# Memory projection of a transformer step on one NeuronCore: VectorE instead of GpSimd adds the squares of the residual, and two intermediate tiles move to PSUM

## The chip, the cores and the metric

The kernel runs on one core of one Trainium2 chip. A core has TensorE (PE) for matmuls, VectorE (DVE) and ScalarE (ACT) for element-wise work, GpSimd (POOL), and SyncE (SP), which here only issues DMAs. Each works through its own queue in order, and they meet at semaphores. SBUF is the working memory, PSUM holds the matmul results in eight banks of 128 x 512 float32. The metric is the device time of one execution in microseconds (us); lower is better. The kernel before takes 2259.66 us, the median of 3 runs (2257.73 to 2259.71).

## The reference

Two transformer blocks run in sequence over 512 tokens of width 1024, all in float32. The change touches one place in the second block: the end of its mixer and the start of its memory cross-attention.

```python
y = hybrid_mixer(rmsnorm_2(h, g[0]), ...)
h = h + rmsnorm_2(y, g[1])                                  # the new residual
y = memory_cross_attention(rmsnorm_2(h, g[2]), rmsnorm_2(mem, mem_norm_g[l]), ...)

def memory_cross_attention(h, mem_n, w_q, w_kv, w_o):
    q = (h @ w_q)                                           # phase "xq"
    k, v = jnp.split(mem_n @ w_kv, 2, axis=-1)              # phase "kv"
    ...

def rmsnorm_2(x, g):
    return x * lax.rsqrt(jnp.mean(x * x, axis=-1, keepdims=True) + EPS) * g
```

The mean of squares runs over the 1024 features of a token. The kernel holds activations as 8 feature tiles of 128 partitions x 512 tokens, so it squares 8 tiles, adds them into one tile (`sqacc`), and lets matmuls against a column of ones sum over the partitions.

## The kernel before

All weights stream from HBM as 324 units of 128 x 1024 float32 (512 KB), four buffers deep (`RING`). Each product is made of three matmuls of split numbers: a weight `w` is split into `w_hi`, which ScalarE writes (`split_hi`, helper line 529), and `w_lo = raw - w_hi`, which GpSimd writes (`split_lo`, line 468). TensorE takes a unit only when its `w_lo` is there (`weights`, line 1715, semaphore `lo_ready`). ScalarE makes `w_hi` of a unit three units ahead, after TensorE has finished the one whose buffers it takes.

The stage in question is phase `kv`, the projection of the 256 memory tokens: 16 units, called 0 to 15 below. Units 0 to 7 give the keys, one feature tile per unit, 24 matmuls of 256 columns (lines 2271 to 2274). Units 8 to 15 give the values, 12 matmuls of 512 columns per unit (`token_tiles`); `stat()` stands between units 11 and 12 and sums `sqacc` over the partitions, and `spread_rs()` behind unit 15 spreads the inverse root. Then phase `xq` begins, eight units of 24 matmuls of 512 columns on the new residual.

While TensorE runs units 0 to 15, the other engines make the new residual out of the mixer's output `yv`, tile by tile, k = 0 to 7:

- VectorE, `next_residual` (lines 1304 to 1326): scales `yv` by gain and inverse root (line 1319), adds it to `resid` (1320), and one tile later writes `x_lo` of the normalised input's low part (`low`, 1311) out of `resid` and `x_hi`.
- ScalarE, `scaled_tile` (558 to 563): writes `x_hi`, then squares the residual tile, into `sqacc` for k = 0, otherwise into one of two halves of `tn`. Between them in its queue it makes `w_hi` and moves the key tile out of PSUM (`kmt`, line 911).
- GpSimd (lines 511 to 519): makes `w_lo` of units 3 to 11, with one `add_square` (line 455, `sqacc += tn`) after each of the splits from unit 5 on, and at last raises `sq_ready`, for which `stat()` waits.

The order on each engine is the order in which the code is written. Two waits tie them: a square for k of 3 or more waits until the square two tiles back is added (`rsq_used`), and ScalarE's last `scaled_tile` waits for all the additions (line 563) before it goes on to `w_hi` of unit 12. The same GpSimd loop `add_squares` is used at two other places of the program, which the change leaves alone.

Of the kernel before, what the change touches and what calls it, by code (L numbers as in the profile page):

```python
# [36 lines left out]
ALU = mybir.AluOpType  # L37
ACT = mybir.ActivationFunctionType
# [4 lines left out]
KT = D // P  # L43
T = 512
# [3 lines left out]
RING = 4  # L48
AHEAD = RING - 1
# [120 lines left out]
U0, N_UNITS = starts(PHASES)  # L170
# [31 lines left out]
def build_program(nc, dram):  # L202
    ctx = ExitStack()
    with ctx:
# [18 lines left out]
        resid = fixed("resid", (P, KT, T))  # L223
# [22 lines left out]
        sqacc = fixed("sqacc", (P, T))  # L246
# [94 lines left out]
        aux = ctx.enter_context(nc.psum_tensor("aux", [P, 6 * T], F32))  # L341
        rs = aux[:, 5 * T:6 * T]
# [5 lines left out]
        def sem(name):  # L348
# [5 lines left out]
        S = {n: sem(n) for n in (  # L354

            "dve_step", "act_step", "pool_step",
            "decay_free", "decay_loaded", "consts_loaded", "x_loaded", "tables_loaded", "consts_ready", "stored",
            "ada0_loaded0", "ada0_loaded1", "ada0_loaded2", "ada0_loaded3", "ada1_loaded", "ada_used",
            "ada_ready", "c_ready_act",
            "sq_ready", "stat_ready", "root_ready", "recip_ready", "rs_ready", "res_ready", "rsq_ready", "rsq_used",  # L360
            "hs_ready", "hrecip_ready", "tap_ready", "tap_used", "normed", "norm_hi", "x_ready",
            "v_ready", "z_ready", "log_ready", "sp_ready", "sp_hi_ready", "sp_split",
# [84 lines left out]
        def _(pool):  # L447
            step = Count(pool, S["pool_step"])
            rsq, used = Count(pool, S["rsq_ready"]), Count(pool, S["rsq_used"])

            def add_square(k):

                rsq.next()
                if k:
                    used.own(nc.gpsimd.tensor_tensor(sqacc[:], sqacc[:], tn[:, k % 2, :], ALU.add))  # L455
                if k == KT - 1:
                    pool.sem_inc(S["sq_ready"], 1)
# [7 lines left out]
            def split_lo(u):  # L465
                s = u.slot(RING)
                pool.wait_ge(hi_ready, (u + 1).val())
                nc.gpsimd.tensor_tensor(w_lo[s][:], raw[s][:], w_hi[s][:].bitcast(F32),  # L468
                                        ALU.subtract).then_inc(lo_ready, 1)

            def split_units(first, end):
                with pool.Fori(0, (end - first) // RING) as i:
                    for j in range(RING):
                        split_lo(At(first + j, i, RING))
# [12 lines left out]
            pool_taps, added = list(POOL_TAPS), [0]  # L487
# [22 lines left out]
            split_units(U0["mix_out"] + RING, U0["kv"])  # L510
            for j in range(AHEAD):
                split_lo(At(U0["kv"] + j))
            for k in range(KT):
                split_lo(At(U0["kv"] + AHEAD + k))
                if k:
                    add_square(k - 1)
            split_lo(At(U0["kv"] + AHEAD + KT))
            add_square(KT - 1)
            split_units(U0["kv"] + AHEAD + KT + 1, U0["up"])
            next_phase(U0["up"], NU)  # L520


# [1 line left out]
        def _(act):  # L524
            step = Count(act, S["act_step"])
            own = {n: Count(act, S[n]) for n in S}
# [25 lines left out]
            def square_tile(k):  # L552

                if k >= 3:
                    own["rsq_used"].next()
                own["rsq_ready"].own(f(tn[:, k % 2, :] if k else sqacc[:], resid[:, k, :], ACT.Square))

            def scaled_tile(k, gain):
                own["res_ready"].next()
                own["norm_hi"].own(f(x_hi[:, k, :], resid[:, k, :], scale=gain[:, k:k + 1]))  # L560
                square_tile(k)
                if k == KT - 1:
                    own["rsq_used"].next(2)

# [170 lines left out]
            for j in range(24):  # L735
# [4 lines left out]
                if j in next_hi:  # L740
                    k = next_hi[j]
# [242 lines left out]
        def _(dve):  # L984
# [319 lines left out]
            def next_residual(y, gain, x_gain):  # L1304


                own["rs_ready"].next()

                def low(k):
                    own["norm_hi"].next()  # L1310
                    own["x_ready"].own(V.scalar_tensor_tensor(x_lo[:, k, :], resid[:, k, :], x_gain[:, k:k + 1],
                                                              x_hi[:, k, :].bitcast(F32), ALU.mult, ALU.subtract))

                for k in range(KT):
                    if y is None:
                        own["res_ready"].own(V.scalar_tensor_tensor(resid[:, k, :], resid[:, k, :], gain[:, k:k + 1], rs,
                                                                    ALU.mult, ALU.mult))
                    else:
                        step.own(V.scalar_tensor_tensor(y[:, k, :], y[:, k, :], gain[:, k:k + 1], rs, ALU.mult, ALU.mult))
                        own["res_ready"].own(V.tensor_tensor(resid[:, k, :], resid[:, k, :], y[:, k, :], ALU.add))  # L1320
                    if k:
                        low(k - 1)
                low(KT - 1)
                own["sq_ready"].skip()
                invert()
                take_rs()
# [1147 lines left out]
```

## Time and profile before

| | |
|---|---|
| time, median of 3 runs | 2259.66 us |
| profiled execution | 2259.86 us, span 2257.7 us |
| mean granted TensorE clock | 0.969 |
| TensorE busy | 2097.1 us (93% of the span) |
| GpSimd busy | 945.8 us (42%) |
| VectorE busy | 989.9 us (44%) |
| ScalarE busy | 921.7 us (41%) |
| chain that ended last | PE 81%, DVE 9%, ACT 5%, issue 2%, POOL 2% |

The profile is one execution, and its times are from the span's start; the stage lies at about 1641 to 1701 us. Busy shares are averages over the whole program, so they say little about a stage of 60 us; what is read there is who waits for whom. An instruction's row shows its start, its length, its engine and line, and in square brackets how long the engine sat idle before it and what ended that. Line 529 is the helper through which ScalarE's operations go, so they are told apart by their tiles.

### The profile page before, as it was taken

Reading aid. Unit: us, or ns where it says so; the run is one execution under the profiler, and the core shown is the slowest. Engines: PE = TensorE matmul, PEld = TensorE weight load, DVE = VectorE, ACT = ScalarE, POOL = GpSimd, SP = SyncE. Lnnn points to the kernel's source line nnn. Section 1 sums busy time; section 2 is a strip of 40 time slices with the busy share of each in tenths; the row PEclk is TensorE's granted clock in tenths of the full one; section 3 lists DMA queues with packets and bytes.
Section 4 is the critical chain, followed back from the end, with each engine's and each line's share of the span. In section 5 each row is a group of like instructions: output and inputs, shape, how many; then the busy total and the mean of one; then the engine's idle time right before and its main releaser. Section 6 shows DMA issues by size and latency. Waiting matters only on the chain.

```text
span 2257.7 us, 27865 instructions
## 1 busy us (share of the span) xinstructions
PE 2097.1 (93%) x9954; PEld 1719.7 (76%) x9954; DVE 989.9 (44%) x1101; ACT 921.7 (41%) x1094; POOL 945.8 (42%) x431
## 2 busy tenths in 40 slices
PE   3999989999999998999999999888889869999996
PEld 3788868787878777888888878787678557887885
DVE  7055532454544556211124377484661364343223
ACT  2366652223232342444422475563352325555421
POOL 3422224243434333444445376572374043444451
PEclk9999999999999999999999999898999979999998
DMA  7311112433333322323333222100333022232331
GB/s 266 94 57 57 57 56 86 153 107 132 116 133 130 111 83 76 93 93 102 93 103 102 87 73 72 50 1 1 119 105 122 10 65 66 93 96 91 111 102 46
DMA packets 56232, 203.69 MB, mean 90 GB/s; under 512 B 6240, under 2 KB 6368, under 8 KB 55904
## 3 DMA queue, kind: packets, MB, share of 16 engines
q1 hardware_dynamic: 56160, 202.70, 27.8%
q8 instruction: 49, 0.80, 0.1%
q14 instruction: 23, 0.19, 0.0%
HBM read 200.57 MB, written 2.10 MB: 90 GB/s over the span
## 4 chain that ended last, share of the span: by engine, by line
PE 81%; DVE 9%; ACT 5%; issue 2%; POOL 2%; DMA 1%; DVEq 0%; ACTq 0%; SPq 0%; POOLq 0%
PE acc L1719 21%; PE acc L1721 20%; PE acc L1720 20%; PE aux L1719 2%; PE aux L1721 2%; PE aux L1720 2%; ACT sp L529 2%; PE acc L1928 2%; PE aux L1776 2%; PE aux L2152 1%; DVE cfy L1375 1%; PE aux L1783 1%; POOL sqacc L455 1%; PE aux L1842 1%; PE acc L2311 1%
## 5 line engine op out<-in xcount | busy, mean ns | idle before, releaser
L468 POOL TENSOR_TENSOR w_lo<-raw,w_hi 128x1024 fp32r<-128x1024 f32 x324 | 796.1, 2460 | 1192.4 <-ACT w_hi L529 1190.9
L1719 PE MATMUL acc<-x_hi,w_hi 128*128 128x512 f32 x1544 | 618.2, 400 | 12.7 <-DVEq L994 3.8
L1720 PE MATMUL acc<-x_lo,w_hi 128*128 128x512 f32 x1544 | 607.3, 393 | 0.0
L1721 PE MATMUL acc<-x_hi,w_lo 128*128 128x512 f32 x1544 | 606.6, 393 | 0.0
L529 ACT ACTIVATE w_hi<-raw 128x1024 fp32r<-128x1024 f32 x324 | 342.7, 1060 | 555.3 <-PE acc L1721 441.1
L1719 PEld LDWEIGHTS acc<-x_hi,w_hi 128*128 128x128 f32 x1544 | 294.1, 190 | 87.7 <-issue 9.1
L1721 PEld LDWEIGHTS acc<-x_hi,w_lo 128*128 128x128 f32 x1544 | 293.5, 190 | 63.1
L1720 PEld LDWEIGHTS acc<-x_lo,w_hi 128*128 128x128 f32 x1544 | 294.0, 190 | 58.8
L529 ACT ACT_TABLE_LOAD x86 | 110.3, 1283 | 54.5 <-DVE tn L1678 20.8
L1678 DVE SCALAR_TENSOR_TENSOR tn<-acc,cols,tn 128x511 f32<-128x511 f32 x88 | 65.9, 749 | 122.1 <-ACT tn L529 115.7
L1025 DVE SCALAR_TENSOR_TENSOR adac<-ada,c_act,adac 128x1024 f32<-128x1024 f32 x42 | 65.7, 1564 | 97.4 <-DMA ada<-in_ada 96.5
L1247 DVE TENSOR_TENSOR ht<-acc,tn 128x512 f32<-128x512 f32 x22 | 15.2, 692 | 182.4 <-PE acc L1721 178.6
L499 POOL TENSOR_TENSOR cfy<-cfy,tn 128x512 f32<-128x512 f32 x48 | 67.0, 1396 | 36.6 <-ACT tn L529 34.5
L1719 PE MATMUL aux<-w_hi,x_hi 128*128 128x512 f32 x192 | 76.1, 396 | 6.5 <-DVE x_lo L1053 5.2
L1720 PE MATMUL aux<-w_lo,x_hi 128*128 128x512 f32 x192 | 75.7, 394 | 0.0
L1721 PE MATMUL aux<-w_hi,x_lo 128*128 128x512 f32 x192 | 75.7, 394 | 0.0
L1719 PE MATMUL acc<-g_hi,w_hi 128*128 128x512 f32 x176 | 69.3, 394 | 0.0
L1719 PE MATMUL acc<-h_hi,w_hi 128*128 128x512 f32 x176 | 69.3, 394 | 0.0
L1721 PE MATMUL acc<-g_hi,w_lo 128*128 128x512 f32 x176 | 69.0, 392 | 0.0
L1721 PE MATMUL acc<-h_hi,w_lo 128*128 128x512 f32 x176 | 69.0, 392 | 0.0
L1720 PE MATMUL acc<-h_lo,w_hi 128*128 128x512 f32 x176 | 68.3, 388 | 0.0
L1720 PE MATMUL acc<-g_lo,w_hi 128*128 128x512 f32 x176 | 68.3, 388 | 0.0
(376 smaller groups left out, 3228.1 us busy)
## 6 DMA issues: line engine op xcount, KB each, us to landing
raw<-in_weights SPq DMA_DIRECT2D x324, 512.0 KB, 3.5
ada<-in_ada SPq DMA_DIRECT2D x48, 512.0 KB, 3.6
resid<-in_x SPq DMA_DIRECT2D x1, 2048.0 KB, 11.7
out<-resid SPq DMA_DIRECT2D x8, 256.0 KB, 2.0
decay<-in_tables SPq DMA_DIRECT2D x4, 256.0 KB, 3.6
memf<-in_mem SPq DMA_DIRECT2D x1, 1024.0 KB, 4.9
angles<-in_tables SPq DMA_DIRECT2D x1, 512.0 KB, 3.5
small<-in_small SPq DMA_DIRECT2D x1, 320.0 KB, 3.8
```

Of the source, the lines that this page charges most:

```text
L455: used.own(nc.gpsimd.tensor_tensor(sqacc[:], sqacc[:], tn[:, k % 2, :], ALU.add))
L468: nc.gpsimd.tensor_tensor(w_lo[s][:], raw[s][:], w_hi[s][:].bitcast(F32), ALU.subtract).then_inc(lo_ready, 1)
L499: tap_used.own(nc.gpsimd.tensor_tensor(cfy[:, n, :], cfy[:, n, :], product(tap_used.at.c), ALU.add))
L529: return nc.scalar.activation(out, in_, func, **kw)
L1025: return V.scalar_tensor_tensor(dst[:], w, c, dst[:], ALU.mult, ALU.add)
L1375: ins = V.scalar_tensor_tensor(y, x, w, y, ALU.mult, ALU.add)
L1678: ins = V.scalar_tensor_tensor(y, bank(t)[:, 0:T - d], w, y, ALU.mult, ALU.add)
L1719: M(out, a_hi, b_hi, start=first, stop=False)
L1720: M(out, a_hi, b_lo, start=False, stop=False)
L1721: return M(out, a_lo, b_hi, start=False, stop=last)
L1776: m = M(aux[:, at_ + b:at_ + b + 1], src[:, b * P:(b + 1) * P], ones[:, 0:1], start=k == 0 and b == 0, stop=k == len(sources) - 1, skip_gr ...
L1928: m = M(bank(t)[:, j * P:T], rv[:, j, e * P:(e + 1) * P], rsc[:, a:a + w], start=j == 0, stop=j == NB - 1)
```

## The change

Four edits, all for this one stage:

1. GpSimd no longer adds the squares: its queue holds only splits in the stage, and its counters skip the semaphores' values.
2. VectorE adds them, in `low(k)`, behind the write of `x_lo`: seven `tensor_tensor` into `sqacc`. It raises `sq_ready` after the last.
3. ScalarE writes the squares for k of 1 and more into PSUM, banks 2 and 3 of `aux` in turn, not into `tn` in SBUF. Its waits are the same, now on VectorE's additions.
4. The scaled output goes to PSUM bank 4 of `aux` (`added`), not back into `yv` in SBUF, and the addition to `resid` reads it there.

```diff
@@ gpsimd
-            for k in range(KT):
-                split_lo(At(U0["kv"] + AHEAD + k))
-                if k:
-                    add_square(k - 1)
-            split_lo(At(U0["kv"] + AHEAD + KT))
-            add_square(KT - 1)
-            split_units(U0["kv"] + AHEAD + KT + 1, U0["up"])
+            rsq.skip(KT)
+            used.skip(KT - 1)
+            split_lo(At(U0["kv"] + AHEAD))
+            split_units(U0["kv"] + RING, U0["up"])
@@ scalar, scaled_tile
-                square_tile(k)
+                if k >= 3:
+                    own["rsq_used"].next()
+                own["rsq_ready"].own(f(aux[:, (2 + k % 2) * T:(3 + k % 2) * T] if k else sqacc[:], resid[:, k, :], ACT.Square))
@@ vector, next_residual
+                own["rsq_ready"].skip(KT)
+                own["rsq_used"].skip(KT - 1)
+                added = aux[:, 4 * T:5 * T]
 
                 def low(k):
                     own["norm_hi"].next()
                     own["x_ready"].own(V.scalar_tensor_tensor(x_lo[:, k, :], ...))
+                    own["rsq_ready"].next()
+                    if k:
+                        own["rsq_used"].own(V.tensor_tensor(sqacc[:], sqacc[:], aux[:, (2 + k % 2) * T:(3 + k % 2) * T], ALU.add))
...
-                        step.own(V.scalar_tensor_tensor(y[:, k, :], y[:, k, :], gain[:, k:k + 1], rs, ALU.mult, ALU.mult))
-                        own["res_ready"].own(V.tensor_tensor(resid[:, k, :], resid[:, k, :], y[:, k, :], ALU.add))
+                        step.own(V.scalar_tensor_tensor(added, y[:, k, :], gain[:, k:k + 1], rs, ALU.mult, ALU.mult))
+                        own["res_ready"].own(V.tensor_tensor(resid[:, k, :], resid[:, k, :], added, ALU.add))
...
                 low(KT - 1)
+                V.sem_inc(S["sq_ready"], 1)
                 own["sq_ready"].skip()
```

GpSimd's queue in the stage before, from unit 5 on (`w_lo_58` is the low half of unit 5, and the numbers 57 to 60 are the four buffers in turn):

```order
L468 TENSOR_TENSOR w_lo_58<-raw_50,w_hi_54 128x1024
L455 TENSOR_TENSOR sqacc<-sqacc,tn 128x512
L468 TENSOR_TENSOR w_lo_59<-raw_51,w_hi_55 128x1024
L455 TENSOR_TENSOR sqacc<-sqacc,tn 128x512
L468 TENSOR_TENSOR w_lo_60<-raw_52,w_hi_56 128x1024
L455 TENSOR_TENSOR sqacc<-sqacc,tn 128x512
L468 TENSOR_TENSOR w_lo_57<-raw_49,w_hi_53 128x1024
```

The same place now, where a loop of four splits runs from unit 4 on:

```order
L468 TENSOR_TENSOR w_lo_57<-raw_49,w_hi_53 128x1024
L467 REGISTER_ALU
L468 TENSOR_TENSOR w_lo_58<-raw_50,w_hi_54 128x1024
L467 REGISTER_ALU
L468 TENSOR_TENSOR w_lo_59<-raw_51,w_hi_55 128x1024
L467 REGISTER_ALU
L468 TENSOR_TENSOR w_lo_60<-raw_52,w_hi_56 128x1024
```

Seven additions are gone from between the splits; register work of the loop stands there in their place.

VectorE's queue before, from the residual tile k = 1 on:

```order
L1319 SCALAR_TENSOR_TENSOR yv<-yv,cols,aux 128x512
L1320 TENSOR_TENSOR resid<-resid,yv 128x512
L1311 SCALAR_TENSOR_TENSOR x_lo<-resid,cols,x_hi 128x512
L1319 SCALAR_TENSOR_TENSOR yv<-yv,cols,aux 128x512
L1320 TENSOR_TENSOR resid<-resid,yv 128x512
L1311 SCALAR_TENSOR_TENSOR x_lo<-resid,cols,x_hi 128x512
L1319 SCALAR_TENSOR_TENSOR yv<-yv,cols,aux 128x512
L1320 TENSOR_TENSOR resid<-resid,yv 128x512
```

And now (the line numbers are those of the changed kernel, in which these operations are lines 1325, 1326, 1313 and, new, 1318):

```order
L1325 SCALAR_TENSOR_TENSOR aux<-yv,cols,aux 128x512
L1326 TENSOR_TENSOR resid<-resid,aux 128x512
L1313 SCALAR_TENSOR_TENSOR x_lo<-resid,cols,x_hi 128x512
L1325 SCALAR_TENSOR_TENSOR aux<-yv,cols,aux 128x512
L1326 TENSOR_TENSOR resid<-resid,aux 128x512
L1313 SCALAR_TENSOR_TENSOR x_lo<-resid,cols,x_hi 128x512
L1318 TENSOR_TENSOR sqacc<-sqacc,aux 128x512
L1325 SCALAR_TENSOR_TENSOR aux<-yv,cols,aux 128x512
L1326 TENSOR_TENSOR resid<-resid,aux 128x512
```

A turn of VectorE has four instructions instead of three from k = 2 on, and `x_lo` is the only one of them left with both tile operands in SBUF.

## Rows read from the trace of the kernel before

**Rows 1.** Chain that ended last: start, length, work.
```profile
1682.46 1.70 POOL sqacc L455
1685.37 2.36 POOL w_lo L468
```

**Rows 2.** Waits, 1639 to 1702: waiting work, releaser, total us, times, longest.
```profile
ACT w_hi L529 <- POOL sqacc L455: 4.3, 1, 4.3
PE aux L1719 <- POOL w_lo L468: 7.0, 5, 1.4
PE acc L1719 <- POOL w_lo L468: 1.1, 1, 1.1
```

**Rows 3.** TensorE in order of time: start, length, instruction, idle before.
```profile
1663.31 0.28 PE L1721 MATMUL acc<-mem_hi,w_lo 128*128 128x256 f32 x1
...
1669.07 0.50 PE L1719 MATMUL aux<-w_hi,mem_hi 128*128 128x512 f32 x1 [1.33 <-POOL w_lo L468]
...
1685.42 0.95 PE L1776 MATMUL aux<-small,sqacc 128*128 128x1 f32 x8
1687.77 0.50 PE L1719 MATMUL aux<-w_hi,mem_hi 128*128 128x512 f32 x1 [1.41 <-POOL w_lo L468]
...
1695.02 0.40 PE L1719 MATMUL aux<-w_hi,mem_hi 128*128 128x512 f32 x1
...
1697.82 0.40 PE L1719 MATMUL aux<-w_hi,mem_hi 128*128 128x512 f32 x1
...
1700.62 1.05 PE L1783 MATMUL aux<-small,rcol 128*128 128x128 f32 x8
1701.42 0.47 PE L1719 MATMUL acc<-x_hi,w_hi 128*128 128x512 f32 x1
```

**Rows 4.** Busy time by stretch; the number behind POOL is the granted clock.
```profile
1646.40:1663.40 17.00, 17.00 (x146) 16.98 (x145) 16.25 (x13) 12.13 (x18) 12.57 (x6) 1.00 0.36 120
...
1689.07:1692.26 3.19, 3.19 (x9) 2.51 (x8) 0.00 (x0) 0.32 (x1) 3.19 (x2) 0.50 0.71 190
```

**Rows 5.** GpSimd in order of time.
```profile
1655.43 1.76 POOL L455 TENSOR_TENSOR sqacc<-sqacc,tn 128x512 f32<-128x512 f32 x1
1657.27 2.74 POOL L468 TENSOR_TENSOR w_lo<-raw,w_hi 128x1024 fp32r<-128x1024 f32 x1
...
1703.27 2.40 POOL L468 TENSOR_TENSOR w_lo<-raw,w_hi 128x1024 fp32r<-128x1024 f32 x1 [1.46 <-ACT w_hi L529]
```

**Rows 6.** ScalarE in order of time.
```profile
1652.84 0.37 ACT L529 ACTIVATE kmt<-acc 128x256 f32<-128x256 f32 x1
...
1654.07 0.63 ACT L529 ACTIVATE tn<-resid 128x512 f32<-128x512 f32 x1
1654.74 1.06 ACT L529 ACTIVATE w_hi<-raw 128x1024 fp32r<-128x1024 f32 x1
1655.71 0.36 ACT L529 ACTIVATE kmt<-acc 128x256 f32<-128x256 f32 x1
```

**Rows 7.** VectorE in order of time.
```profile
1646.74 0.75 DVE L1319 SCALAR_TENSOR_TENSOR yv<-yv,cols,aux 128x512 f32<-128x512 f32 x1 [5.01 <-PE aux L1783]
1647.52 2.90 DVE L1320 TENSOR_TENSOR resid<-resid,yv 128x512 f32<-128x512 f32 x1
...
1651.96 0.75 DVE L1311 SCALAR_TENSOR_TENSOR x_lo<-resid,cols,x_hi 128x512 fp32r<-128x512 f32 x1
```

**Rows 8.** Tiles of VectorE: line, form, count: shortest/median/longest ns, first and last start.
```profile
L1320 DVE TENSOR_TENSOR resid<-resid,yv x8: 692/1974/2899, 1647.5 to 1676.6; 128x512 f32<-128x512 f32 x8
L1311 DVE SCALAR_TENSOR_TENSOR x_lo<-resid,cols,x_hi x8: 751/1672/2732, 1652.0 to 1680.3; 128x512 fp32r<-128x512 f32 x8
L1319 DVE SCALAR_TENSOR_TENSOR yv<-yv,cols,aux x8: 748/748/749, 1646.7 to 1675.8; 128x512 f32<-128x512 f32 x8
L1531 DVE TENSOR_TENSOR xm<-xm,aux x20: 686/689/690, 1462.7 to 1514.3; 128x512 f32<-128x512 f32 x20
L1449 DVE TENSOR_TENSOR acc<-acc,spare x12: 699/700/700, 1329.5 to 1414.4; 128x512 f32<-128x512 f32 x12
```

## The prediction

> **What bounds the kernel now.** I read the chain of waits first: from 1653 to 1688 us it does not run over TensorE but over GpSimd, where a split and an addition of squares follow each other [rows 1]. The waits say who pays: TensorE stood 7.0 us in five waits and 1.1 us in a sixth for `w_lo`, and ScalarE once 4.3 us for the last addition [rows 2]. Outside this stage the change moves nothing, so the question is how much earlier phase `xq` can begin than at 1701.42 us [rows 3].
>
> GpSimd's period before is one split and one addition. A split alone takes 2.40 us and an addition 1.76, but split and addition in turn take 2.74 + 1.76, 4.5 us together [rows 5]: the split is stretched by 0.34. VectorE shows the other half of the same thing. Where both tile operands are in SBUF, an instruction of 0.69 or 0.75 us takes 1.97 or 1.67 in the median; where one is in PSUM (lines 1319, 1531), shortest and longest differ by at most 4 ns [rows 8]. So the two engines shut each other out, and only for operations with two SBUF operands.
>
> TensorE needs a unit every 2.8 us. Units 8 to 15 are 12 matmuls each, and between 1695.02 and 1697.82 lie twelve: 2.80 us. Units 1 to 6 fill 1646.4 to 1663.43 (the last matmul starts at 1663.31, and they follow at 0.12): 2.83 each. 4.5 us of GpSimd against 2.8 of TensorE is why TensorE starves once its lead of three units is used up, at 1663.43.
>
> **The ceiling of the gain.** If TensorE never waited after 1663.43, unit 7 would take 2.83, units 8 to 15 8 x 2.80 = 22.40, the sum over partitions 0.95 and the spreading 0.80 (1700.62 to 1701.42) [rows 3]. That is 26.98 us, and `xq` would begin at 1690.4, 11.0 us earlier. Of the 11.0, 1.65 is not waiting: from unit 12 to the spreading it took 12.85 us where 11.20 do, because from 1689.07 to 1692.26 the granted clock was 0.50, the 1.2 GHz level, just after the row of waits. With TensorE full from 1646.4 to 1663.4 it was 1.00 [rows 4]. I count it as gained, since the waits ahead of it go.
>
> **The change part by part.**
>
> *GpSimd.* Seven additions of 1.76 go, and their stretching of the splits in part. What is left is one split per unit: 2.40 alone, 2.74 when VectorE is in the way, both under 2.80. The loop's register work stands between splits at 1703.27 too, and the split there is 2.40 [rows 5]; I cost it at nothing, its cover being some 2.5 us of lead per unit.
>
> *ScalarE.* Its turn in the stage is 2.87 us, kmt to kmt [rows 6], so now it and TensorE (2.83) set the pace together; 0.04 a unit over seven units is 0.3 us, inside the lead. Its squares now land in PSUM, which no row before shows for ScalarE. The same square into SBUF takes 0.63. As ends I take 0.36, the key tile with half the columns, and 1.06, the `w_hi` with twice the columns [rows 6], and as value 0.63, the row of the same operation. At 0.36 nothing changes in the layout below, at 1.06 `xq` begins 1.8 us later.
>
> *VectorE.* Its turn becomes scale 0.75, add to the residual 0.69, `x_lo` 0.75, add square 0.69, and four gaps of 0.03 to 0.04: 3.0 us. The form "SBUF and PSUM in, SBUF out" takes 0.69 (line 1531), "PSUM out" 0.70 (line 1449) [rows 8]. For the scaling, which now also writes PSUM, the ends are 0.70 (line 1449, which does so) and 0.76 (its own 0.75 and the 0.01 by which 1449 lies above 1531), and the value is 0.75. The residual's addition loses its waits, 1.97 to 0.69; `x_lo` keeps its own.
>
> *Laid out from 1646.74*, when VectorE gets the inverse root [rows 7]: eight turns of 3.02 less the missing addition of square 0 end at 1670.2. Added are the waits that remain: `x_lo` 0 waits 0.9 for ScalarE's `x_hi`; `x_lo` 1 asks in the middle of the split of unit 5 and waits 1.2; `x_lo` 7 asks just after the split of unit 11 has begun and waits 1.4; small ones make 0.4. The last addition ends at 1674.1, where it was 1684.15. `x_lo` 2 to 6 fall into the 0.4 us between two splits, unit by unit.
>
> *The wait that takes the old one's place.* ScalarE holds the `w_hi` of unit 12 until the last addition is done. From there: `w_hi` 1.06, split 2.40, hand-overs 0.2, in all 3.7, so TensorE has unit 12 at 1677.8. It wants it at 1663.43 + 2.83 + 4 x 2.80 + 0.95 = 1678.4. The margin is 0.6 us: this is the tight place, and every microsecond that the last addition is later than 1674.7 is lost one for one. For the units before, the split is ready 2.4 to 2.8 us ahead of TensorE. `stat()` itself wants the additions only at 1677.4.
>
> *Downstream.* `xq` and all behind it begin earlier by the same amount and find the same state. The last splits before `xq` (unit 16 is wanted at 1690.4) end at 1687.5.
>
> *Sum.* 11.0 less 0.6, for one of the turns that just miss a gap between splits (a miss costs up to 2.4 us there, but it moves the last `x_lo` out of its own wait of 1.4): 10.4 us. The profiled execution took 2259.86 us, its span 2257.7; 2259.86 - 10.4 = 2249.5. The median is 0.2 under the profiled execution: 2249.3.
>
> A page of the Trainium skill speaks against the change: "VectorE: DVE Perf Modes", section "The TRN2 errata", has a VectorE operation cost 58 cycles plus its elements from SBUF and 120 plus its elements from PSUM, at 0.96 GHz. This case's trace does not agree for two-operand forms: 689 ns with PSUM (line 1531), 692 for the shortest with none (line 1320) [rows 8]. By the page the two additions of a turn would take 0.755 each and the time would be that of the first rival.
>
> **The rivals.**
>
> *Longer turns, missed gaps.* If the additions on PSUM take 0.75, as the scaling does, not 0.69, a turn is 3.15 against ScalarE's 2.87. VectorE then falls out of the gap between two splits at `x_lo` 4 and again at 6, waits out a split each time, and the last addition ends at 1677.4. Unit 12 starts at 1681.1, 2.7 late: gain 8.3, time 2251.4. The far end is a lock-step: ScalarE waits for the residual tile, its `w_hi` ends 2.5 later, the split 2.5 after that, and `x_lo` waits for that split. A turn P then satisfies P = (5.0 - P) + 0.75 + 0.69 + 0.75 + 0.69 + 0.1, so P = 4.0; eight turns end at 1678.7, unit 12 starts at 1682.4: gain 7.0, 2252.7. For it: GpSimd is busy 2.4 of 2.87 us, so a gap is small. Against it: the forms of [rows 8].
>
> *The time is given back.* TensorE's faster pace wants 512 KB every 2.8 us. If the weights came later than ScalarE asks, the gain would go. To cancel it within the bound of no change they would have to be over 6 us late, and a load is released when the split of four units before is done, about 8 us before its `w_hi` is due. Or ScalarE's writes to PSUM are dearer than the end that I took. Time about 2257.
>
> *Slower: operands in PSUM do not free VectorE.* If an addition with one operand in PSUM still waits for GpSimd, the residual's addition and the square's stay at 1.97. Then every turn waits out one split: 3.0 + 2.4 = 5.4 us, eight turns from 1646.74 end near 1690, unit 12 starts at 1694.6, `xq` at 1694.6 + 11.2 + 0.8 = 1706.6: 5.2 later than before, 2264.9. It decides from a turn of about 4.8 us on, where unit 12 starts at 1689. For it: seven more instructions on VectorE, and the median of 1.97 before. Against it: the 28 executions of lines 1319 and 1531 within 4 ns, those of 1319 in this very stage [rows 8].
>
> **How the numbers follow.** The forecast has 0.72: `xq` at 1690.4 to 1692.0 and perhaps a half-clock stretch that stays (1.65), which is 2248.4 to 2251.2. Longer turns 0.16 (2251.2 to 2254.5), given back 0.07, slower 0.05. The range is 2247.4 to 2254.5, with a microsecond of spread between runs below; it leaves out the two last cases. About 0.2%, 4.5 us, is what a measurement of this kernel can tell from no change: faster 0.88, same 0.07, slower 0.05.
>
> **What would show it.** In the changed profile: GpSimd has no addition between 1650 and 1690 and its splits come every 2.8 to 2.9 us; the residual's addition is 0.69 to 0.70 in all eight; `x_lo` is still stretched, in two or three of eight; TensorE has no wait for `w_lo` in units 7 to 11, and at unit 12 none or under 1 us; the granted clock stays 1.00 from 1646 to the end of the stage; `xq` begins at 1690.4 to 1692. It is wrong if TensorE waits at unit 12 for more than 1.5 us (the margin is mis-sized), if the residual's addition is stretched (the slower rival), or if ScalarE's square is over 0.9 us.

## The result, and the profile after

The changed kernel takes 2245.26 us, the median of 4 runs (2244.34 to 2246.15); the kernel before took 2258.69 in 4 runs (2257.33 to 2259.71) that include the three shown above. The ratio is 0.994, 95% interval 0.9924 to 0.9955: the interval lies wholly under 1, so the change is faster by 0.6%, small but clear of noise. The time lies 4.0 us under the forecast of 2249.3 and 2.1 under the range's lower end. The profiled execution took 2246.15, its span 2244.3; before it was 2259.86 and 2257.7. One run of the kernel before, at 7381.75 us where all others lie between 2253 and 2263, is left out of every figure below.

TensorE in order of time, as in [rows 3] (start, length, instruction, idle before):

```profile
1676.39 0.50 PE L1726 MATMUL aux<-w_hi,mem_hi 128*128 128x512 f32 x1 [0.27 <-POOL w_lo L468]
...
1687.69 1.05 PE L1790 MATMUL aux<-small,rcol 128*128 128x128 f32 x8
1688.50 0.47 PE L1726 MATMUL acc<-x_hi,w_hi 128*128 128x512 f32 x1
```

This is the only wait for `w_lo` that is left, 0.27 us at unit 12, where six waits made 8.1 us [rows 2]. The stage, from the scaling that starts it to `xq`'s first matmul, goes from 54.68 us (1646.74 to 1701.42) to 44.04 (1644.46 to 1688.50). The stretches of the stage show no half clock (the number behind POOL is the granted clock; compare 0.50 in [rows 4]):

```profile
1644.40:1661.40 17.00, 17.00 (x147) 17.00 (x146) 14.68 (x19) 13.99 (x21) 12.42 (x5) 1.00 0.46 146
1661.40:1676.40 15.00, 14.73 (x81) 12.47 (x79) 10.90 (x13) 10.36 (x16) 10.35 (x6) 1.00 0.46 144
1676.40:1688.50 12.10, 12.10 (x56) 9.88 (x57) 0.18 (x1) 5.41 (x7) 12.10 (x6) 1.00 0.65 205
```

VectorE's tiles, as in [rows 8] (here shortest/median/longest ns):

```profile
L1326 DVE TENSOR_TENSOR resid<-resid,aux x8: 686/686/687, 1645.2 to 1669.0; 128x512 f32<-128x512 f32 x8
L1313 DVE SCALAR_TENSOR_TENSOR x_lo<-resid,cols,x_hi x8: 752/752/2914, 1648.5 to 1671.3; 128x512 fp32r<-128x512 f32 x8
L1325 DVE SCALAR_TENSOR_TENSOR aux<-yv,cols,aux x8: 754/756/756, 1644.5 to 1668.2; 128x512 f32<-128x512 f32 x8
L1318 DVE TENSOR_TENSOR sqacc<-sqacc,aux x7: 686/686/689, 1653.3 to 1672.0; 128x512 f32<-128x512 f32 x7
```

The residual's addition fell from 1974 ns in the median to 686, and its longest is 1 ns above its shortest. Only `x_lo`, which still reads two SBUF tiles, is stretched, and only in two of eight:

```profile
1651.41 1.82 DVE L1313 SCALAR_TENSOR_TENSOR x_lo<-resid,cols,x_hi 128x512 fp32r<-128x512 f32 x1 [0.60 <-ACT x_hi L526]
...
1664.56 2.91 DVE L1313 SCALAR_TENSOR_TENSOR x_lo<-resid,cols,x_hi 128x512 fp32r<-128x512 f32 x1
...
1672.04 0.69 DVE L1318 TENSOR_TENSOR sqacc<-sqacc,aux 128x512 f32<-128x512 f32 x1
```

The last addition ends at 1672.73, 28.3 us after the start of the stage, where it took 37.4. ScalarE, as in [rows 6]:

```profile
1650.10 0.36 ACT L526 ACTIVATE kmt<-acc 128x256 f32<-128x256 f32 x1
...
1651.34 0.60 ACT L526 ACTIVATE aux<-resid 128x512 f32<-128x512 f32 x1
...
1652.94 0.37 ACT L526 ACTIVATE kmt<-acc 128x256 f32<-128x256 f32 x1
```

**Where 13.7 us of the profiled execution went.** The stage gives 10.64. It also began 2.28 earlier, though nothing ahead of it was edited; what follows `xq`'s first matmul took 555.80 instead of 556.28, 0.48 less; and the time outside the span is 0.31 less. The last three were in no term of the forecast; e1, e2, e10 and e11 ask whether they belong to the change.

### The profile page after: what moved, and what is told of

It is laid out like the page before. It is cut to its first block, busy times and chain, and to the rows that moved or that the text cites. A ratio compares the mean times of both kernels' runs of the same rounds, so it can differ in the third digit from the quotient of the medians.

```text
span 2244.3 us, 27877 instructions
## 1 busy us (share of the span) xinstructions
PE 2091.8 (93%) x9954; PEld 1716.7 (76%) x9954; DVE 980.2 (44%) x1108; ACT 921.4 (41%) x1094; POOL 933.1 (42%) x424
## 4 chain that ended last, share of the span: by engine, by line
PE 80%; DVE 9%; ACT 5%; issue 3%; POOL 2%; DMA 1%; DVEq 0%; ACTq 0%; SPq 0%; POOLq 0%
PE acc L1726 21%; PE acc L1728 20%; PE acc L1727 20%; PE aux L1726 2%; PE aux L1728 2%; PE aux L1727 2%; ACT sp L526 2%; PE acc L1935 2%; PE aux L1783 1%; PE aux L2159 1%; DVE cfy L1382 1%; POOL w_lo L468 1%; PE aux L1790 1%; PE aux L1849 1%; DMA ada<-in_ada 1%
```

## The experiments

Each kernel was timed beside the kernel before, except the last two, which are single profiled executions. e1 to e4 ran on one chip, e5 to e8 on a second, e9 to e11 on a third; the kernel before had medians of 2258.2, 2257.7 and 2258.7 there. "Stage" is measured as above. In the edits shown, `...` stands for lines left out.

### e1 and e2: both kernels again

No edit.

> The kernel before, unchanged, as a second program. The stage gain explains 10.6 of the 13.4 us (from the arrival of the inverse root to the start of phase xq 54.7 us before, 44.0 after); 2.3 us more were already there when the stage began, in code that the change leaves alone. Theory A (executions differ by themselves): this kernel is within 0.1% of the kernel before, and its profile begins the stage at a time other than 1646.7, by up to 2.5 us either way, through half-clock stretches and DMA waits that lie elsewhere; its stage is still 54.0 to 55.0 long. Rival B (the change shifts the whole program for good): its profile begins the stage at 1646.7 +- 0.3.

> The changed kernel, unchanged, beside the same runs. Theory A: the difference in time lies between 10.6 and 13.4 us and its profile may begin the stage anywhere from 1644.4 to 1647; stage 44.0 +- 0.3 long. Rival B: the difference is 13.0 to 13.8 again and the stage begins at 1644.4 +- 0.3 again.

Measured: the kernel before again 2258.64 us (12 runs, 2254.34 to 2262.98), ratio 1.0006 [0.9997, 1.0015]; the changed kernel 2246.83 (5 runs, 2244.5 to 2248.75), ratio 0.9955 [0.9942, 0.9968]. Stages 54.73 and 44.06, within 0.05 of the first profiles; the wait at unit 12 is 0.29. The stage starts at 1649.96 and 1644.58. The first is not rival B's 1646.7, but it is 3.2 us away from it where theory A had up to 2.5, and the kernel before is again the later of the two, so e10 and e11 ask once more. The stage reproduces to hundredths, and the whole does not: all 71 runs of the kernel before, those of the later experiments included, lie between 2252.99 and 2262.98, with median 2258.19, and 9 of the changed one between 2244.34 and 2248.75, median 2246.15. The difference of these medians is 12.0.

### e3: VectorE adds, both tiles stay in SBUF

```
-  own["rsq_ready"].own(f(aux[:, (2 + k % 2) * T:(3 + k % 2) * T] if k else sqacc[:], resid[:, k, :], ACT.Square))
+  own["rsq_ready"].own(f(tn[:, k % 2, :] if k else sqacc[:], resid[:, k, :], ACT.Square))
...
-  own["rsq_used"].own(V.tensor_tensor(sqacc[:], sqacc[:], aux[:, (2 + k % 2) * T:(3 + k % 2) * T], ALU.add))
+  own["rsq_used"].own(V.tensor_tensor(sqacc[:], sqacc[:], tn[:, k % 2, :], ALU.add))
...
-  step.own(V.scalar_tensor_tensor(added, y[:, k, :], gain[:, k:k + 1], rs, ALU.mult, ALU.mult))
-  own["res_ready"].own(V.tensor_tensor(resid[:, k, :], resid[:, k, :], added, ALU.add))
+  step.own(V.scalar_tensor_tensor(y[:, k, :], y[:, k, :], gain[:, k:k + 1], rs, ALU.mult, ALU.mult))
+  own["res_ready"].own(V.tensor_tensor(resid[:, k, :], resid[:, k, :], y[:, k, :], ALU.add))
```

> VectorE adds the squares, but squares and scaled output stay in SBUF (tn and yv). Theory (homes matter: every VectorE operation with two SBUF operands waits for GpSimd's split): the residual addition and the square addition are stretched to about 2 us in the median, a turn is about 5 us, and the stage is no shorter than before: laid out with the durations of the trace, xq begins 1.3 us later than before; time -3 to +4 us against the kernel before. Rival (what counts is only that GpSimd's queue has no additions): at least 8 us faster than before.

Measured: 2259.67 (11 runs), ratio 1.001 [1.0, 1.0019]; stage 58.08, 3.4 longer than before. Three rows of its trace, GpSimd and VectorE in order of time, and one of TensorE:

```profile
1666.49 2.48 POOL L468 TENSOR_TENSOR w_lo<-raw,w_hi 128x1024 fp32r<-128x1024 f32 x1 [0.33 <-ACT w_hi L526]
1666.76 2.77 DVE L1317 TENSOR_TENSOR sqacc<-sqacc,tn 128x512 f32<-128x512 f32 x1
...
1676.32 0.68 PE L1725 MATMUL aux<-w_hi,mem_hi 128*128 128x512 f32 x1 [3.87 <-POOL w_lo L468]
```

The square's addition starts 0.27 us into a split and ends at 1669.53, 0.56 after the split's end at 1668.97: it waits for nearly all of it. VectorE's pattern is two turns to 10.2 us, one with both `x_lo` and the addition of the square stretched to 2.7 to 2.8, one without. Moving the additions to VectorE is thus worth nothing by itself: it needs the homes in PSUM. (It does not follow that the homes alone carry the gain; see e4.) The third rival of the prediction had VectorE wait out a split in every turn, 5.4 us; this kernel waits out two in every second turn and comes to 5.1.

### e4: GpSimd still adds, only the scaled output goes to PSUM

```
+  added = aux[:, 4 * T:5 * T]
...
-  step.own(V.scalar_tensor_tensor(y[:, k, :], y[:, k, :], gain[:, k:k + 1], rs, ALU.mult, ALU.mult))
-  own["res_ready"].own(V.tensor_tensor(resid[:, k, :], resid[:, k, :], y[:, k, :], ALU.add))
+  step.own(V.scalar_tensor_tensor(added, y[:, k, :], gain[:, k:k + 1], rs, ALU.mult, ALU.mult))
+  own["res_ready"].own(V.tensor_tensor(resid[:, k, :], resid[:, k, :], added, ALU.add))
```

> The kernel before, with the scaled output alone in PSUM; GpSimd still adds the squares. Theory (GpSimd's queue of split and addition sets the pace): its pace stays near 4.2 to 4.5 us per unit, xq begins 2 to 3.5 us earlier than before, through the first addition to the residual that no longer waits 2.2 us. Rival (port waits of VectorE set the pace): residual additions at 0.69 and over 6 us faster than before.

Measured: 2254.62 (11 runs), ratio 0.9988 [0.9979, 0.9997]; stage 52.22, 2.5 shorter than before. GpSimd and VectorE in e4:

```profile
1655.34 1.76 POOL L455 TENSOR_TENSOR sqacc<-sqacc,tn 128x512 f32<-128x512 f32 x1
1657.17 2.41 POOL L468 TENSOR_TENSOR w_lo<-raw,w_hi 128x1024 fp32r<-128x1024 f32 x1
...
1676.50 1.29 POOL L455 TENSOR_TENSOR sqacc<-sqacc,tn 128x512 f32<-128x512 f32 x1
```

```profile
1653.27 2.65 DVE L1312 SCALAR_TENSOR_TENSOR x_lo<-resid,cols,x_hi 128x512 fp32r<-128x512 f32 x1
...
1657.48 2.66 DVE L1312 SCALAR_TENSOR_TENSOR x_lo<-resid,cols,x_hi 128x512 fp32r<-128x512 f32 x1
```

and VectorE in the kernel before, for [rows 5]:

```profile
1653.53 2.50 DVE L1320 TENSOR_TENSOR resid<-resid,yv 128x512 f32<-128x512 f32 x1
1656.07 1.67 DVE L1311 SCALAR_TENSOR_TENSOR x_lo<-resid,cols,x_hi 128x512 fp32r<-128x512 f32 x1
```

These rows show what stretches GpSimd: a VectorE operation with two SBUF tiles that is still running when GpSimd's operation starts. Before, `x_lo` runs 0.47 us into the split of 1657.27, and that split takes 2.74; in e4 nothing of the kind is running at 1657.17 (`x_lo` starts inside the split and is itself held), and the split takes 2.41. The square's addition takes 1.76 in both, because something with two SBUF tiles reaches 0.6 us into it each time, the residual's addition before and `x_lo` in e4; the last addition, with nothing beside it, takes 1.29. So with the residual's addition out of the way GpSimd's turn is still 4.2 us against TensorE's 2.8. One home alone brings 2.5 us of the stage, the move alone (e3) loses 3.4; the gain of 10.6 needs the move and the homes. GpSimd adding with both homes in PSUM was not run.

### e5 and e6: one home in PSUM each, VectorE adds

e5 keeps `added` in PSUM and puts the squares back into `tn`; e6 keeps the squares in PSUM and puts the scaled output back into `yv`. The lines are those of e3, its first two pairs in e5, its last two in e6.

> The changed kernel, but with the residual's squares left in SBUF (only the scaled sublayer output has its home in PSUM, VectorE adds the squares). This leaves the output as it is. My theory (two SBUF tile operands shut VectorE and GpSimd out of each other, one PSUM operand frees the pair): the residual's additions stay at 0.69 us in all eight, the square's additions and x_lo are stretched in turns, so VectorE falls behind from about the third turn on; laid out by the durations of the changed kernel's profile the stage is some 4.2 us longer than the changed kernel's 44.05, that is 48.3 (range 46.5 to 50.5), TensorE waits in units 8 to 12 for some 2 to 4 us in all, against the changed kernel's 0.3. Time about 2250 to 2251, some 6 us under the kernel before. Rival (only the residual's addition matters, since it is the one that starts in the middle of a split; the square's addition is hidden): stage 44 to 44.5, time as the changed kernel, about 2246.

> The changed kernel, but with the scaled sublayer output left in SBUF (only the squares have their home in PSUM, VectorE adds them). The output is as it is. My theory: the square's additions stay at 0.69 us, the residual's additions and x_lo are stretched; laid out by the same durations the stage is some 7.4 us longer than the changed kernel's, 51.4 (range 49 to 54), so between the changed kernel and the one before (54.7), and TensorE waits 5 us or more in units 8 to 12. Time about 2253, some 3 us under the kernel before. Rival (it makes no difference which of the two operands moves): stage equal to that of the version with the squares in SBUF within 0.5 us.

Measured: e5 2249.73 (7 runs), ratio 0.9967 [0.9956, 0.9979], stage 49.37; e6 2253.82 (12 runs), ratio 0.9981 [0.9973, 0.999], stage 52.41. VectorE's tiles in e5:

```profile
L1326 DVE TENSOR_TENSOR resid<-resid,aux x8: 686/686/687, 1645.1 to 1672.3; 128x512 f32<-128x512 f32 x8
L1313 DVE SCALAR_TENSOR_TENSOR x_lo<-resid,cols,x_hi x8: 751/1308/1930, 1648.3 to 1675.1; 128x512 fp32r<-128x512 f32 x8
L1318 DVE TENSOR_TENSOR sqacc<-sqacc,tn x7: 691/691/2833, 1653.1 to 1675.9; 128x512 f32<-128x512 f32 x7
```

and in e6:

```profile
L1325 DVE TENSOR_TENSOR resid<-resid,yv x8: 692/1250/2894, 1643.5 to 1673.6; 128x512 f32<-128x512 f32 x8
L1317 DVE TENSOR_TENSOR sqacc<-sqacc,aux x7: 686/686/689, 1654.8 to 1677.2; 128x512 f32<-128x512 f32 x7
```

In each kernel the operation whose one operand is in PSUM stays within 3 ns of 686, and those with two SBUF tiles vary. With VectorE adding, the stage is 58.1 with no home, 52.4 with the squares' home, 49.4 with the scaled output's, 44.05 with both: 5.7 and 8.7 alone, 14.0 together, so the two nearly add up. Both rivals fall (that the home of the squares is worth nothing, and that the two are worth the same). One part of the expectation for e5 missed: the square's addition is stretched in one of seven only, and it is `x_lo` that pays in six of eight. The one stretched addition, 2.83 us at 1653.08 where the changed kernel has 0.69, is enough to throw every later `x_lo` but the last out of the gap between splits. I had laid out 48.3 and 51.4; each came out 1.0 longer. In e5 TensorE waits 3.67 us in three waits, and behind the last of them the clock falls (busy time by stretch, as above):

```profile
1676.00:1680.00 4.00, 1.73 (x12) 1.34 (x10) 0.56 (x1) 3.36 (x4) 2.22 (x1) 0.97 0.19 79
1680.00:1684.00 4.00, 3.82 (x11) 3.06 (x12) 0.00 (x0) 1.73 (x3) 4.00 (x3) 0.61 0.53 146
```

0.39 of 4 us is 1.6 us of granted clock that the layout did not have, as much as the kernel before paid at unit 12 [rows 4]; e6 has such stretches too, behind two waits. How the 1.0 is made up was not worked out. In e5 the whole fell by more than the stage, 8.5 us from the median of all runs before against 5.3, because what follows the stage took 554.17 us there (see what stays open).

### e7: the same cure in the tiles of mix_out, xo and down

```
+  squared = aux[:, 2 * T:3 * T]
+  step.own(V.tensor_tensor(squared, bank(t), dst, ALU.mult))
   free(t)
-  step.own(V.tensor_tensor(sqt[:], dst, dst, ALU.mult))
-  step.own(V.tensor_tensor(sqacc[:], sqacc[:], sqt[:], ALU.add))
+  step.own(V.tensor_tensor(sqacc[:], sqacc[:], squared, ALU.add))
```

> The changed kernel, and besides in each sublayer tile of the phases mix_out, xo and down VectorE squares from the matmul's PSUM bank and the copy into another PSUM bank, and adds the squares from there, so that neither has two SBUF operands. What is computed is the same. My theory (what is stretched is only what has two SBUF tile operands, wherever it stands): in mix_out, where squares and their additions take up to 2.83 and 2.77 us at 1626.66 and 1629.52 in the changed kernel's profile, they fall to 0.69 to 0.70, and TensorE's 5.9 us ahead of the sum over partitions at 1637 shrink by 3 to 3.7 us; in xo and down the operations after the last tile stand alone and give nothing, under 0.3 us. The stage of the memory projection stays 44.05 within 0.1. Total 3 to 4 us under the changed kernel, about 2242.5. Rival (the wait ahead of the sum is set by the last tile's chain of copy, square and addition, not by VectorE's backlog): 0.5 us or less, time as the changed kernel.

Measured: 2240.85 (5 runs), ratio 0.9924 [0.9911, 0.9938], 5.3 us under the changed kernel's 2246.15; the stage of the memory projection is 44.08. TensorE's two long waits of `mix_out` in the changed kernel:

```profile
1605.89 1.22 PE L1790 MATMUL aux<-small,rcol 128*128 128x128 f32 x4 [4.65 <-DVE rcol L1616]
1637.02 1.87 PE L1783 MATMUL aux<-small,sqacc 128*128 128x1 f32 x8 [5.88 <-DVEq L1606]
```

and in e7:

```profile
1604.93 1.11 PE L1791 MATMUL aux<-small,rcol 128*128 128x128 f32 x4 [2.63 <-DVE rcol L1617]
1631.80 1.35 PE L1784 MATMUL aux<-small,sqacc 128*128 128x1 f32 x8 [2.76 <-DVEq L1607]
```

The mechanism holds and the size was too small: I had looked at the second wait alone (3.1 us less, as expected) and missed that a stretched addition stands ahead of the first too (2.0 less). What follows the stage, where the phases `xo` and `down` have the same edit, took 556.58, no less than before, also as expected.

### e8: TensorE adds the squares between xo and up

Built on e7:

```
+  for k in range(KT):
+      own["rsq_ready"].next()
+      src = tn[:, k % 2, :] if k else sqacc[:]
+      for b in range(NB):
+          m = M(aux[:, 4 * T + b:4 * T + b + 1], src[:, b * P:(b + 1) * P], ones[:, 0:1],
                start=k == 0 and b == 0, stop=k == KT - 1, skip_group_check=True)
...
```

GpSimd's seven additions go; ScalarE takes the root from bank 4.

> The version with the sublayer squares in PSUM, and besides between xo and up TensorE adds up the residual's squares tile by tile with matmuls of one column into PSUM, where GpSimd added seven times 1.6 us from 1833.88 to 1845.37 and TensorE stood 15.6 us ahead of the sum. What is computed is the same up to the order of additions. My theory (GpSimd's backlog and its stretching of the residual's additions, 0.86 against 0.69, set that wait): 3 to 3.5 us less than the version it builds on, about 2239. Rival (that wait is set by the chain of normalisation ahead of it, the root, the reciprocal and eight residual additions, which GpSimd only follows): under 1.5 us less. A second rival: the small matmuls come at a lower granted clock, and what is gained there goes in the first units of up.

Measured: 2239.5 (5 runs, 2238.36 to 2242.89), ratio 0.9916 [0.9903, 0.9929], 1.35 under e7 (2239.5 to 2243.15), which those ranges do not set apart. The traces do: from the first scaling to the first matmul of `up` it is 22.60 us in e7 and 21.36 in e8, 1.24 less. The 3 to 3.5 that I expected did not come. TensorE in e8:

```profile
1830.28 1.87 PE L2335 MATMUL aux<-small,sqacc 128*128 128x1 f32 x8 [2.36 <-ACT sqacc L525]
1832.01 12.09 PE L2335 MATMUL aux<-small,tn 128*128 128x1 f32 x56
```

and the stretch around it, 14 us at a granted clock of 0.50, the 1.2 GHz level:

```profile
1830.00:1844.00 14.00, 13.72 (x64) 13.72 (x64) 9.61 (x14) 4.64 (x8) 0.00 (x0) 0.50 0.00 0
```

Eight small matmuls a tile (the trace has two for each of the four in the code) take 12.09 / 7 = 1.73 us, more than GpSimd's 1.64 a turn that they replace and more than VectorE's 1.51 a turn. So the pace did not improve: the last of them ends 16.1 us after the first scaling, GpSimd's last addition in e7 15.3. What was gained is the separate sum over partitions behind that addition, 1.86 us in e7, which is no longer needed. The first rival's size fits (under 1.5) but not its reason, and the second named the clock but put its price into `up`: the bound moved to TensorE's sums themselves. A price in `up` can't be told either way: from its first matmul to its next wait it takes 15.61 us in e8, 14.94 in e7, 15.65 in the changed kernel.

### e9: GpSimd and VectorE share the additions between xo and up

Built on e7:

```
-  add_squares()
+  for k in range(KT - 2):
+      add_square(k)
...
-  step.own(V.scalar_tensor_tensor(y[:, k, :], y[:, k, :], gain[:, k:k + 1], rs, ALU.mult, ALU.mult))
-  own["res_ready"].own(V.tensor_tensor(resid[:, k, :], resid[:, k, :], y[:, k, :], ALU.add))
+  step.own(V.scalar_tensor_tensor(added, y[:, k, :], gain[:, k:k + 1], rs, ALU.mult, ALU.mult))
+  own["res_ready"].own(V.tensor_tensor(resid[:, k, :], resid[:, k, :], added, ALU.add))
...
+  for k in range(KT - 2, KT):
+      own["rsq_ready"].next()
+      own["rsq_used"].own(V.tensor_tensor(sqacc[:], sqacc[:], tn[:, k % 2, :], ALU.add))
...
```

> The version with the sublayer squares in PSUM (without TensorE's sums), and between xo and up the scaled sublayer output goes to PSUM and VectorE adds the last two of the residual's eight squares, behind its last residual addition, where GpSimd added all of them. What is computed is the same. My theory (GpSimd's row of additions, 1.64 us each from 1833.88 to 1845.37 in the changed kernel's profile, ends that wait; and VectorE is stretched beside it, 0.86 for 0.69): all eight residual additions take 0.69, GpSimd ends its five some 8.1 us after it begins, VectorE ends the last two 1.8 to 2.1 us earlier than GpSimd did, TensorE's wait ahead of the second sum falls from 15.6 to about 13.6, and the time is 2 us under the version that it builds on (2240.85), 2239. Rival (the sum is bound by the turns of scaling and addition ahead of it, not by GpSimd): the 0.85 of the unstretched additions alone, or nothing.

Measured: 2237.11 (4 runs, 2233.47 to 2238.42), ratio 0.9902 [0.9885, 0.9919], the lowest median of all. GpSimd and TensorE in e7:

```profile
1828.92 11.49 POOL L455 TENSOR_TENSOR sqacc<-sqacc,tn 128x512 f32<-128x512 f32 x7 [12.81 <-ACT tn L526]
...
1840.50 1.86 PE L1784 MATMUL aux<-small,sqacc 128*128 128x1 f32 x8 [15.55 <-POOLq L457]
```

and in e9:

```profile
1833.67 1.27 POOL L455 TENSOR_TENSOR sqacc<-sqacc,tn 128x512 f32<-128x512 f32 x1 [0.24 <-ACT tn L527]
...
1837.46 1.86 PE L1792 MATMUL aux<-small,sqacc 128*128 128x1 f32 x8 [13.79 <-DVEq L1349]
```

The wait falls by 1.8, as expected, but half of the reason was wrong. I took GpSimd's 1.64 us for its own pace; without VectorE's additions of two SBUF tiles beside it, it takes 1.27 and waits 0.24 for ScalarE each time. So the home in PSUM had already freed GpSimd, and the shared additions bring little beyond it: GpSimd would have ended the seventh at about 1838.0 (the last square ends at 1836.55, GpSimd begins 0.14 later as after the other squares, and takes 1.27), VectorE ended it at 1837.35, an estimate of 0.6. That part was not run alone. The median is 3.7 under e7's where 2 was expected; from the first scaling to `up` the traces give 1.82, and the rest is not shown to come from the edit.

### e10 and e11: the kernel before, a third and a fourth profile

> The kernel before, a third profiled execution. What it is for: by the two profiles so far the memory projection's stage of this kernel begins at 1646.7 and 1650.0 us, in the six kernels that share the code ahead of it at 1642.7 to 1644.6. If that is a difference between executions and not between kernels, the stage is again 54.7 us within 0.1, what follows it 556 within 1, and its start lies anywhere between 1641 and 1650, so the span is 611 us plus the start. The median time of all runs of this kernel so far, 2257.7, then stands for a start of 1644.6. Rival (the kernel before begins its stage later than the others, for a reason in the code): start again at 1646.5 or later.

> The kernel before, a fourth profiled execution, for the same question: if executions differ and not kernels, at least one of the third and the fourth has a start under 1646; if the kernel before has something of its own ahead of the stage, neither has.

Measured: stages 54.67 and 54.67, starts 1644.52 and 1648.82, what follows 556.11 in both. By the rule set down, executions differ: with 1646.74 and 1649.96 the four starts of this one kernel span 5.4 us, and the third lies with the others' 1642.7 to 1644.6. One place where they part lies about 200 us ahead of the stage. TensorE in the first profile of the kernel before:

```profile
1413.65 1.97 PE L2089 MATMUL aux<-small,qkvf 128*128 128x128 f32 x8 [4.03 <-DVE xt L1429]
...
1457.27 0.98 PE L2152 MATMUL aux<-xm,bt 128*128 128x128 f32 x3 [3.74 <-ACT xm L529]
```

```profile
1410.00:1430.00 20.00, 16.35 (x81) 15.08 (x82) 11.16 (x15) 10.72 (x16) 11.25 (x7) 0.73 0.22 76
1430.00:1450.00 20.00, 20.00 (x107) 17.23 (x107) 10.03 (x14) 8.49 (x10) 9.90 (x6) 0.93 0.17 53
```

and in e10:

```profile
1414.37 1.97 PE L2089 MATMUL aux<-small,qkvf 128*128 128x128 f32 x8 [4.00 <-DVE xt L1429]
...
1454.97 3.29 PE L2152 MATMUL aux<-xm,bt 128*128 128x128 f32 x13 [3.74 <-ACT xm L529]
```

```profile
1410.00:1430.00 20.00, 16.00 (x89) 14.09 (x88) 13.34 (x18) 12.96 (x18) 12.33 (x8) 0.85 0.24 79
1430.00:1450.00 20.00, 20.00 (x112) 17.21 (x110) 8.53 (x12) 6.95 (x9) 11.66 (x7) 0.98 0.18 53
```

The same waits, 4.0 and 3.7 us, but 43.6 us from one to the other against 40.6: (0.27 - 0.15 + 0.07 - 0.02) x 20 = 3.4 us less of granted clock. That is not the whole of it. e1 and e11, the two late ones, have the short distance, 40.7 and 40.6, and stand 5.2 and 4.3 us behind e10 at the first of these waits already (1419.62 and 1418.69). The changed kernel has 40.5 in its first profile and 43.6 in e2, and starts the stage within 0.12 of the same time. From the second wait to the stage it is 189.5 to 189.6 in all six profiles of the two kernels. So the spread arises ahead of 1460 us, in more than one place, and only this place was looked into.

## Why the prediction was right or wrong

**The ceiling and the sum: right.** Ceiling 43.7 us from the start of the stage (1690.4 less 1646.74), measured 44.04; gain 10.4 forecast, 10.64 in the first pair of profiles, 10.6 to 10.7 in every pair of the four before and two after.

**The half clock at unit 12: right.** The stage has 1.00 throughout. e5 shows the reverse: with waits left, the clock falls there again.

**GpSimd: right in its pace.** A unit every 2.84. Its splits take 2.40 to 2.93, not 2.40 to 2.74: the longest has 0.66 us of `x_lo` in it. And the prediction took 1.76 for a lone addition of squares; that is a stretched one too, alone it takes 1.27 (e9). Nothing in the sum hung on it, as the additions go.

**ScalarE: nearly.** Turn 2.84 for 2.87, the square into PSUM 0.60 for 0.63, both to the good.

**VectorE's turn: right.** 1655.50 to 1658.52 is 3.02, as laid out. The scaling took the upper end, 0.756, the additions 0.686.

**Which `x_lo` miss a gap: wrong tile, right price.** `x_lo` 1 lost 1.07 (laid out 1.2). `x_lo` 7, which I had wait 1.4, waited for nothing, and `x_lo` 5 lost 2.16 instead. GpSimd and VectorE show why (the row of three has splits that start at 1658.79, 1661.63 and 1664.53):

```profile
1655.95 2.57 POOL L468 TENSOR_TENSOR w_lo<-raw,w_hi 128x1024 fp32r<-128x1024 f32 x1 [0.42 <-ACT w_hi L526]
1658.79 8.14 POOL L468 TENSOR_TENSOR w_lo<-raw,w_hi 128x1024 fp32r<-128x1024 f32 x3 [0.27 <-ACT w_hi L526]
```

```profile
1661.54 0.75 DVE L1313 SCALAR_TENSOR_TENSOR x_lo<-resid,cols,x_hi 128x512 fp32r<-128x512 f32 x1
```

VectorE's turn of 3.02 is 0.18 longer than the 2.84 between splits, so each `x_lo` comes that much later against them: `x_lo` 4 starts 0.09 ahead of a split, `x_lo` 5 (1664.56) 0.03 behind the next. Both periods stood in the prediction, and "`x_lo` 2 to 6 fall into the 0.4 us" did not add up their difference. The sum had this exchange (a miss of up to 2.4 that takes the last out of its 1.4), and 27.4 + 2.16 - 1.40 = 28.2 against 28.3 measured.

**The margin at unit 12: used up.** 0.6 was laid out; the last addition came 0.9 later than laid out, and TensorE waited 0.27. From that addition to unit 12 it took 3.66, 3.7 in the forecast.

**"Longer turns, missed gaps": did not come.** The additions on PSUM took 686 ns, not 750. The Trainium skill, page "VectorE: DVE Perf Modes", section "The TRN2 errata", puts the fixed cost at 120 cycles from PSUM and 58 from SBUF. The prediction's 0.755 is 0.69 and these 62 cycles, and two-operand forms do not bear them out: 686 ns with one tile in PSUM, 691 with both in SBUF (lines 1326 and 1318 of e5). The same section of the Trainium skill says that its 58 is too low and has 691 ns for a float32 `tensor_tensor` of 512 columns, which e5 agrees with.

**"Operands in PSUM do not free VectorE": refuted** by the 686/686/687 of the changed kernel, and e3 shows what it would have been. The Trainium skill, page "SBUF — State Buffer", section "Who interferes with whom", has a VectorE instruction with two SBUF inputs contend with a GpSimd instruction that reads SBUF, and one with at most one such input (outside the modes that use both ports) not; e3 to e6 agree, tile by tile.

**"The time is given back": did not come.** TensorE had no wait in the stage but the 0.27; ScalarE waited 3.3 us for loads, in two waits that no one else felt. What follows took 556.11 to 556.28 in the four profiles of the kernel before and 555.80 and 555.86 in the two after.

**Slips in the working.** Three figures do not follow from their own terms. The slower rival: eight turns to 1690 and 3.7 make unit 12 start at 1693.7, not 1694.6, and the time 2264.0. The forecast's own span: `xq` at 1690.4 is 2248.7, not 2248.4, and `xq` at 1692.0 with 1.65 on top is 2251.9, not 2251.2. None moves the forecast of 2249.3.

**The step that failed is the range's lower end,** "with a microsecond of spread between runs below", together with the base from which the 10.4 us were taken, one profiled execution and the median of three runs. The range was made of what the stage could do, and about one microsecond was left for all else. Against the measured 2245.26, the forecast of 2249.3 is off by 4.0: from the start of the stage 2.28, from the tail 0.48, from the time outside the span 0.31, from the stage 0.24, and the remaining 0.7 from the median's place against the profiled execution. The first is spread between executions: e10, the same kernel as before, starts the stage at 1644.52, the changed one at 1644.46. Three runs within 2 us hid it: 71 runs span 10 us, and their median, 2258.19, lies 1.5 under the three's. From 2258.19 the same 10.4 gives 2247.8, inside the range; 9 runs of the changed kernel gave 2246.15, still 1.25 under its lower end. So the base is about half of the miss against all runs (1.5 of 3.15), and the rest is in what stays open.

**What stays open.** Of 12.0 us between the long medians the stage has 10.6, the tail 0.3 and the time outside the span 0.4. Neither of the last two was forecast. What follows the stage repeats within 0.2 us for each of the two kernels, but in e4, e5 and e6, whose code there is the same, it is 557.40, 554.17 and 555.65, so its 0.3 can't be put down to the change; what moves it was not looked into. The time outside the span is 2.11 to 2.23 us in all runs with a span on record of the kernels in which GpSimd adds in this stage (before, e4) and 1.73 to 1.85 in all of those where it does not, so it goes with that move; why, no run here shows. The 0.7 that is left may be spread of nine runs.

## What to carry to other kernels

Look at each VectorE operation beside GpSimd for the count of its SBUF tile operands, not for its length: where shortest and longest are far apart, give one operand a home in a free PSUM bank before you move work to VectorE; here the move alone lost 3.4 us of the stage, the home of one tile alone brought 2.5, and both homes with the move 10.6. One such place has siblings; search the profile for the same form in other stages (e7 took another 5.3 us out of `mix_out` with three lines). Where two engines run at nearly the same period, lay out how they drift against each other: 0.18 us a turn was enough for a missed gap. And before a range is set around a small change, take the spread from many runs of the kernel before, not from three: here three spanned 2 us and 71 spanned 10. The clock column of the stages that the change leaves alone gives a warning: stretches at half clock behind waits there can differ between executions without any edit.

## What the runs showed of the hardware

- A VectorE operation with two SBUF tiles that starts 0.27 us into a GpSimd split ends 0.56 us after it (e3). The stretching is mutual, and goes by what is already running: GpSimd's addition of a 128 x 512 tile takes 1.27 us with no such operation running at its start (e9) and 1.76 where one runs 0.6 us into it (e4); its split 2.41 (e4) and, with 0.47 us, 2.74 (before).
- ScalarE's square of 128 x 512 float32 takes 0.60 us into PSUM and 0.63 into SBUF; VectorE's scaling 0.756 and 0.748.
- Eight matmuls of one column against 128 x 128 float32 blocks take 1.73 us at the 1.2 GHz level; the granted clock was 0.50 in all 14 us of them (e8).
- Between the same two waits of 4.0 and 3.7 us, two executions of one kernel took 43.6 us and 40.6, with 3.4 us less of granted clock in the longer (before and e10).
